# Neighbourhood attention on halves of the grid, with its values regrouped by transfers; a weight unit split in halves in the second mixer

## The reference

```python
s = einsum('brjqhd,brjuvhd->brjhquv', qg, k_win) * scale + bias
s = where(col_ok, s, -inf)      # 16 columns around the query's own
p = softmax(s over all kept keys)
o = einsum('brjhquv,brjuvhd->brjqhd', p, v_win)
```

## Time and profile before

| | before |
|---|---|
| median of 3 runs (lowest to highest) | 1637.62 us (1637.54 to 1637.75) |
| profiled execution, its own time | 1637.62 us |
| its span, first to last instruction | 1635.8 us |
| TensorE busy | 1625.7 us |
| VectorE, ScalarE, GpSimd busy | 937.8, 793.2, 149.5 us |
| mean granted TensorE clock | 0.999 |

### The profile page before, as it was taken

How to read it: one execution, slowest core, us unless ns; L and a number is a source line. 1 busy time by engine, 2 the same in 40 slices (tenths; PEclk the granted TensorE clock), 3 DMA queues, 4 the chain that set the end, 5 groups by cost and what they waited for, 6 DMA issues and landing times.

```text
span 1635.8 us, 20418 instructions
## 1 busy us (share of the span) xinstructions
PE 1625.7 (99%) x7642; PEld 1346.8 (82%) x7642; DVE 937.8 (57%) x900; ACT 793.2 (48%) x927; POOL 149.5 (9%) x197
## 2 busy tenths in 40 slices
PE   9999999999999999999999999999999999999998
PEld 7888888888888888888888888888888888888887
DVE  6454655675544645465566554477654457774455
ACT  6443455544444534445464443466544446554444
POOL 1001211011000000121101010031100002210000
PEclk9999999999999999999999999999999999999999
DMA  8777554447565667755444666561666564366562
GB/s 282 253 213 222 196 180 143 162 158 226 182 199 174 194 223 209 221 205 180 136 162 160 200 223 199 191 195 68 206 202 199 177 217 159 100 201 196 173 205 90
DMA packets 210099, 305.99 MB, mean 187 GB/s; under 512 B 11044, under 2 KB 153784, under 8 KB 210040
## 3 DMA queue, kind: packets, MB, share of 16 engines
q1 hardware_dynamic: 208616, 302.82, 56.7%
q0 software_dynamic: 1120, 1.86, 0.5%
q10 hardware_dynamic: 304, 0.50, 0.1%
HBM read 304.07 MB, written 2.88 MB: 188 GB/s over the span
## 4 chain that ended last, share of the span: by engine, by line
PE 96%; DVE 1%; POOL 1%; ACT 1%; SPq 0%; DMA 0%; issue 0%; POOLq 0%; ACTq 0%; DVEq 0%
PE pg L1860 20%; PE pg L1862 20%; PE pg L1861 20%; PE acc L1860 9%; PE acc L1862 9%; PE acc L1861 9%; PE pg L1979 2%; PE pg L1873 1%; PE acc L2065 1%; PE acc L2084 1%; DMA raw<-in_ffn_w_in 0%; PE acc L2072 0%; POOL work L856 0%; PE acc L2262 0%; PE acc L2220 0%
## 5 line engine op out<-in xcount | busy, mean ns | idle before, releaser
L1288 DVE TENSOR_TENSOR wlo<-raw,whi 128x2048 fp32r<-128x2048 f32 (+1 forms) x269 | 616.9, 2294 | 477.8 <-ACT whi L887 477.7
L887 ACT ACTIVATE whi<-raw 128x2048 fp32r<-128x2048 f32 (+1 forms) x269 | 513.2, 1909 | 323.8 <-PE acc L1862 157.6
L1860 PE MATMUL pg<-whi,xTh 128*128 128x512 f32 (+1 forms) x1456 | 576.5, 396 | 1.5 <-DVE xTl L1752 1.1
L1862 PE MATMUL pg<-whi,xTl 128*128 128x512 f32 (+1 forms) x1456 | 566.5, 389 | 0.0
L1861 PE MATMUL pg<-wlo,xTh 128*128 128x512 f32 (+1 forms) x1456 | 565.9, 389 | 0.0
L1860 PEld LDWEIGHTS pg<-whi,xTh 128*128 128x128 f32 x1456 | 273.7, 188 | 59.6 <-issue 1.7
L1862 PEld LDWEIGHTS pg<-whi,xTl 128*128 128x128 f32 x1456 | 273.4, 188 | 56.4
L1861 PEld LDWEIGHTS pg<-wlo,xTh 128*128 128x128 f32 x1456 | 273.8, 188 | 55.1 <-issue 1.4
L1860 PE MATMUL acc<-whi,bTh 128*128 128x512 f32 (+1 forms) x572 | 228.6, 400 | 0.0
L1862 PE MATMUL acc<-whi,bTl 128*128 128x512 f32 (+1 forms) x572 | 222.9, 390 | 0.0
L1861 PE MATMUL acc<-wlo,bTh 128*128 128x512 f32 (+1 forms) x572 | 221.8, 388 | 0.0
(11 more groups left out here) (238 smaller groups left out, 1074.6 us busy)
## 6 DMA issues: line engine op xcount, KB each, us to landing
raw<-in_ffn_w_in SPq DMA_DIRECT2D x172, 512.0 KB, 4.8
raw<-in_ffn_w_out SPq DMA_DIRECT2D x88, 512.0 KB, 4.3
raw<-in_w_gate_up SPq DMA_DIRECT2D x88, 512.0 KB, 4.6
raw<-in_mix_w_in SPq DMA_DIRECT2D x64, 512.0 KB, 4.4
raw<-in_w_down SPq DMA_DIRECT2D x44, 512.0 KB, 4.1
raw<-in_w_in SPq DMA_DIRECT2D x24, 512.0 KB, 4.6
raw<-in_mix_w_o SPq DMA_DIRECT2D x16, 512.0 KB, 4.4
raw<-in_w_o SPq DMA_DIRECT2D x16, 512.0 KB, 4.5
```

The source lines that it names most:

```text
L887: act_e.activation(whi[:, slot, 0:cols], raw[:, slot, 0:cols], ACT.Copy).then_inc(s.w_hi_ready, 1)
L1288: v.tensor_tensor(wlo[:, slot, 0:cols], raw[:, slot, 0:cols], f32(whi[:, slot, 0:cols]), ALU.subtract)\
L1860: pe.matmul(dst, xh, wh, start=first and i == 0, stop=False)
L1862: mm = pe.matmul(dst, xl, wh, start=False, stop=last and i == len(pairs) - 1)
```

## The change

In the first block's mixer a token tile of the attention is no longer 128 tokens in order (two grid rows), but one half of the grid: 4 rows by 32 columns. Such a half sees 4 x 40 keys instead of 256.

- `scores` has 2 x 4 x 40 = 320 columns (read from `kD` in pieces of 40), bias, maximum and exponentials too. The q copies write the halves' order; the mask and the bias transfers follow it (eight transfers per layer where there were four).
- The values are regrouped by transfers on SP's queue: `halve_values(t)` copies the 128 own keys of a half to `v_half` (4 transfers) and the 32 keys beyond it, for both heads of a pair on a block diagonal, to `v_edge` (8 transfers), which GpSimd zeroes first. SP issues the first after unit 11's load, the second after unit 13's and after the first `attend`.
- `scale(i-1)` on VectorE, between `refills(i+8)` and `add_gate_bias`, multiplies the probabilities by the inverse sums and sorts them in own keys (256 columns for the pair) and beyond (64). `probs_T` then waits for that and has three transposes. ScalarE copies the result in two pieces.
- `attend` has the values stationary and the turned probabilities moving: two products (128 keys, 64 channels, 128 queries) and one (64 rows for both heads' edges, 128 channels). The output comes out turned, so `normalise`, `attention_T` and `o_nat` go. ScalarE's and VectorE's `attended(t)` make `oTh` and `oTl`: t = 0 at the head of step 6, t = 1 after the loop.

In the second mixer the last addition of the convolution's second tile moves from GpSimd to VectorE, ahead of the split of unit 11. Unit 13 is split in two halves, ScalarE's both ahead of three of the group squares, VectorE's ahead of `scale_pair(1, .)` and between the two `pair_lo(1, .)`. The first half takes the place of count 12, and TensorE waits for the second half only in the middle of the first half block.

```diff
@@ SP, mixer_a
+                def halve_values(t):
+                    first, edge = t * HALF_W, (HALF_W, HALF_W - BEYOND)[t]
+                    for row in range(GRID_H):
+                        at, src = row % 2 * GRID_W, v_nat[:, row // 2, :]
+                        sp.dma_start(v_half[row * HALF_W:(row + 1) * HALF_W, t, :], src[at + first:at + first + HALF_W, :])\
+                            .then_inc(s.v_half_landed, 16)
+                    for row in range(GRID_H):
+                        at, src = row % 2 * GRID_W + edge, v_nat[:, row // 2, :]
+                        for e in range(2):
+                            to = e * EDGE + row * BEYOND
+                            dst = v_edge[to:to + BEYOND, t, :].rearrange("p (k e n) -> p e k n", k=4, e=2)[:, e]
+                            sp.dma_start(dst, src[at:at + BEYOND, :].rearrange("p (k e n) -> p e k n", k=4, e=2)[:, e])\
+                                .then_inc(s.v_half_landed, 16)
...
+                    if b == 5:
+                        sp.wait_ge(s.v_sb, 2 * l + 2)
+                        sp.wait_ge(s.qkT_tr, 4 * l + 4)
+                        sp.wait_ge(s.kd_zeroed, l + 1)
+                        halve_values(0)
+                    if b == 6:
+                        sp.wait_ge(s.na_o_done, 8 * l + 1)
+                        halve_values(1)
@@ VectorE, mixer_a
+                def scale(i):
+                    t, hp = i // 4, i % 4
+                    v.wait_ge(s.na_exp, 8 * l + i + 1)
+                    pair = na_inv[:, t, 2 * hp:2 * hp + 2]
+                    v.reciprocal(pair, na_sum[:, t, 2 * hp:2 * hp + 2]).then_inc(s.na_rinv, 1)
+                    v.wait_ge(s.na_rinv, 8 * l + i + 1)
+                    if i >= 1:
+                        v.wait_ge(s.naPT_done, 8 * l + i)
+                    p4 = probs[:, i % 2, :].rearrange("p (e r c) -> p e r c", e=2, r=GRID_H)
+                    own, beyond = ((0, HALF_W), (BEYOND, 0))[t]
+                    factors = pair.unsqueeze(2).unsqueeze(3)
+                    v.tensor_tensor(scaled[:, 0:T].rearrange("p (e r c) -> p e r c", e=2, r=GRID_H), p4[:, :, :, own:own + HALF_W],
+                                    factors.to_broadcast([P, 2, GRID_H, HALF_W]), ALU.mult)
+                    v.tensor_tensor(scaled[:, T:].rearrange("p (e r c) -> p e r c", e=2, r=GRID_H), p4[:, :, :, beyond:beyond + BEYOND],
+                                    factors.to_broadcast([P, 2, GRID_H, BEYOND]), ALU.mult).then_inc(s.na_scaled, 1)
...
                     if i == 6:
-                        normalise(0)
+                        attended(0)
                     if i < 9:
                         refills(i + 8)
+                    if 1 <= i <= 8:
+                        scale(i - 1)
@@ TensorE, mixer_a
-                    pe.matmul(acc[0][:, :], qT[:, hp, tok(t)], kD[:, hp, :, :], start=True, stop=True).then_inc(s.na_scores, 1)
+                    pe.matmul(acc[0][:, 0:2 * GRID_H * SEEN], qT[:, hp, tok(t)], seen(kD[:, hp, :, :], t), start=True, stop=True)\
+                        .then_inc(s.na_scores, 1)
 
                 def probs_T(i):
-                    pe.wait_ge(s.na_exp, 8 * l + i + 1)
+                    pe.wait_ge(s.na_scaled, 8 * l + i + 1)
                     for e in range(2):
-                        for kt in range(TT):
-                            at = e * T + kt * P
-                            tr = pe.transpose(acc[2][:, at:at + P], probs[:, i % 2, at:at + P], ident[:, :])
-                    tr.then_inc(s.naPT_done, 1)
+                        pe.transpose(acc[2][:, tok(e)], scaled[:, tok(e)], ident[:, :])
+                    pe.transpose(acc[2][0:2 * EDGE, T:T + P], scaled[:, T:T + 2 * EDGE], ident[:, :]).then_inc(s.naPT_done, 1)
...
-                            mm = pe.matmul(acc[3][:, h * NA_D:(h + 1) * NA_D], probsT[:, i % 2, at:at + P],
-                                           v_nat[:, kt, h * NA_D:(h + 1) * NA_D], start=kt == 0, stop=kt == 1)
-                    mm.then_inc(s.na_o_done, 1)
+                        pe.matmul(acc[3][e * NA_D:(e + 1) * NA_D, tok(hp)], v_half[:, t, h * NA_D:(h + 1) * NA_D],
+                                  probsT[:, i % 2, tok(e)], start=True, stop=False)
+                    pe.matmul(acc[3][:, tok(hp)], v_edge[:, t, tok(hp)], probsT[0:2 * EDGE, i % 2, T:T + P], start=False, stop=True)\
+                        .then_inc(s.na_o_done, 1)
@@ VectorE, mixer_b
+                v.wait_ge(s.conv_taps, 6 * l + 6)
+                v.tensor_tensor(convT[:, :, tok(1)], convT[:, :, tok(1)], taps[0], ALU.add).then_inc(s.conv_T, 1)
                 refills(11)
                 mla_out(1)
                 conv_out(1)
+                half_unit(13, 0)
                 scale_pair(1, 0)
                 scale_pair(1, 1)
-                skip(12)
-                refills(13)
                 pair_lo(1, 0)
+                half_unit(13, 1)
                 pair_lo(1, 1)
```

More of the change, by code:

```diff
@@ L101, in first_constants @@
     out[:, CA_DFT_C:CA_MASK] = np.concatenate([np.concatenate([even, odd]), np.concatenate([odd, even])], 1)
[L102 to L105, removed]
+    for half in range(TT):
+        col = half * HALF_W + np.arange(P) % HALF_W
+        start = np.clip(col - NA_COLS // 2, 0, GRID_W - NA_COLS)[:, None]
+        key = FIRST_SEEN[half] + np.arange(SEEN)[None, :]
+        at = CA_MASK + half * SEEN
+        out[:, at:at + SEEN] = np.where((key >= start) & (key < start + NA_COLS), 0.0, MASKED)
     return out
@@ L392, in build @@
         q_nat, k_nat = area(4096, TT, BANK), area(5120, TT, BANK)
-        o_nat = q_nat
+        v_half = area(4096, TT, BANK)
+        v_edge = work[0:2 * EDGE, 9216:9216 + TT * BANK].rearrange("p (t n) -> p t n", t=TT)
         v_nat, uf = area(6144, TT, BANK), area(7168, TT, BANK)
@@ L618, in attention_bias @@
                     sp.wait_ge(s.rpb_spread, LOADED * NA_DR * (l + 1))
[L619 to L623, removed]
+                    column = DEPTH * NA_H * NA_DR * GRID_W
+                    for row in (2 * r, 2 * r + 1):
+                        src = bass.AP(tensor=spread.tensor,
+                                      offset=t * HALF_W * column + l * (NA_H * NA_DR * GRID_W) + (GRID_H - 1 - row) * GRID_W,
+                                      ap=[[column, HALF_W], [NA_DR * GRID_W, NA_H], [1, T]])
+                        sp.dma_start(bias[HALF_W * row:HALF_W * (row + 1), t, :, :], src).then_inc(s.bias_landed, 16)
                 ffn("ffn1_w_in", "ffn1_w_out", l, r1,
@@ L1072, in mixer_a @@
                     sigmoid(3, t)
+                attended(1)
                 refills(17, 18, 19)
-                for t in range(TT):
-                    act_e.wait_ge(s.oT_tr, 2 * l + t + 1)
-                    copy(oTh[:, :, tok(t)], acc[2 * t][:, :].rearrange("p (c n) -> p c n", c=4), s.oT_hi)
                 refills(20, 21)
@@ L1464, in mixer_a @@
                 refills(3, 4, 5, 6)
-                def heads_T(n, dst, t, bank):
-                    v.wait_ge(s.qkT_tr, 4 * l + n + 1)
-                    v.tensor_copy(dst[:, :, tok(t)], bank[:, :].rearrange("p (c n) -> p c n", c=4)).then_inc(s.qkT_sb, 1)
                 for t in range(TT):
-                    heads_T(t, qT, t, acc[t])
+                    v.wait_ge(s.qkT_tr, 4 * l + t + 1)
+                    rows = acc[t][:, :].rearrange("p (k r h c) -> p h k r c", k=4, h=TT, c=HALF_W)
+                    for half in range(TT):
+                        at = half * P + t * 2 * HALF_W
+                        last = v.tensor_copy(qT[:, :, at:at + 2 * HALF_W].rearrange("p k (r c) -> p k r c", c=HALF_W), rows[:, half])
+                    last.then_inc(s.qkT_sb, 1)
                 v.wait_ge(s.kd_zeroed, l + 1)
@@ L1880, in split_ready, with half_block @@
                 pe.wait_ge(s.w_lo_ready, unit(slot, rnd) + 4)
-            def half_block(t, half, slot, rnd, n, bank, amid=None, first=0):
+            def half_block(t, half, slot, rnd, n, bank, amid=None, first=0, ready=None):
                 if t == 0:
-                    split_ready(slot, rnd)
+                    split_ready(*(ready or (slot, rnd)))
                 for k0 in range(0, 4, 2):
@@ L2382, in project @@
                         pe.wait_ge(s.xT_lo_ready, 4 * (o + 1) + 2 * k + t + 1)
-                    mm = half_block(t, 1 - k, u % SLOTS, rnd + u // SLOTS, BANK, out_b[n][t], amid, first=1)
+                    ready = None
+                    if u == 13 and t == 0:
+                        ready = (u - 1) % SLOTS, rnd + (u - 1) // SLOTS
+                        amid = lambda: split_ready(u % SLOTS, rnd + u // SLOTS)
+                    mm = half_block(t, 1 - k, u % SLOTS, rnd + u // SLOTS, BANK, out_b[n][t], amid, first=1, ready=ready)
                     if t == 1:
```

101 lines of the change are left out of this document (61 added, 40 removed).

## The result

The changed kernel takes 1647.22 us, median of 6 runs (1645.68 to 1649.14), beside 1637.58 us for the kernel before, 6 runs (1637.33 to 1637.97): a ratio of 1.0062, 95% interval 1.0051 to 1.0072. It is slower by 0.6%, above the forecast of 1638.5 and above the range of 1633.5 to 1644.

What follows compares the result with a forecast made beforehand. TensorE's instruction stream was taken to bound the kernel: 11.7 us of its work go and 14.5 us of waits come (+2.8), the second mixer gains 1.9, so 1637.6 + 2.8 - 1.9 = 1638.5 us, range 1633.5 to 1644.

Steps and rivals of the forecast that it cites:

- even steps: Even steps of the attention loop: TensorE waits 1.8 us per layer in all, added up from several small gaps.
- steps 3, 5 and 7: Odd steps of the attention loop: TensorE waits 1.2 us in each for the scaling queued behind VectorE's split.
- The price of the first scaling, 0.76 us: VectorE's scaling of the probabilities: reciprocal 0.20, 128x256 multiplication 0.34 to the next start, 128x64 one 0.21.
- First turn ... 244.76: Start of a layer's first probability transposes in the attention loop: 244.76 us, 1.21 later than before.
- Rival (3): Attention loop: scaling costs 1.1 instead of 0.76, or as much is lost in semaphores, every turn; 1642.9 us, chance 0.15.
- 6 x 0.108 = 0.65: Attend on TensorE: three products of 128 columns, six instructions at 0.108 us each, against 0.84 before.
- now three in 0.33: Transposes of probabilities on TensorE: three in 0.33 us per unit, where four took 0.44.
- 8.17 + x: Turn-to-turn time from even to odd step, before 7.62 + x: +0.55 us each; x is Fourier work after the turn.
- the second mixer's gain: Second mixer: moving the convolution addition and halving unit 13 gain 0.95 us per layer, 1.9 us in all.
- rival 4: Value regrouping on SyncE's queue lands late: at 1.5 us per transfer, 6 us late per layer, 1650.5 us; chance 0.06.
- Rival (1): Attention loop: scaling is ready before TensorE comes, so only the removed work counts; 1624 us, chance 0.05.
- removed work: TensorE work saved by scores, transposes, attend and dropped output turns: 5.84 us per layer, 11.7 for both.

Runs made afterwards that it cites:

- scale_first: The changed kernel with VectorE scaling unit i-1 ahead of the split of unit i+8 in every step; 1628.33 us, ratio 0.9943.
- pool_late: The changed kernel with GpSimd's Fourier additions held back until the layer's first scaling is done; 1640.36 us, ratio 1.0016.
- experiment 2: `pool_late` plus an unused VectorE maximum over 1792 bias columns ahead of each layer's first scaling; 1646.91 us. One more low-clock stretch was estimated at 1.6 us.
- wide_own_t1: `scale_first` with edge product and third transpose zero-padded to 128 rows, and own-key products to 128 columns in units 4 to 7; 1625.47 us, ratio 0.9925.

## Why the prediction was wrong

The mechanism was right: the scaling behind the split makes TensorE wait, the even steps too, and the gain in work is eaten. `scale_first` shows it with no wait and 18.9 us less. The waits are 14.5 us as forecast, but by chance: per layer 3.68 at the first turn where 1.85 was forecast, 0.96 in steps 3, 5 and 7 where 1.2 was, and 0.69 in even steps where 1.8 was (TensorE came later there, by the third term below). Three terms were wrong:

- **The price of the first scaling, 0.76 us.** "First turn ... 244.76" took the scaling from VectorE rows that stand alone. In step 1 GpSimd's Fourier additions run at that moment, and the two instructions take 2.5 us to the end. The first turn is 1.85 late per layer: 3.7 us. Rival (3) had a scaling of 1.1 in every turn as its case; it was dearer than that, but in one turn per layer. `pool_late` removes this and its consequence. The trace of before had the sign: in step 1 GpSimd's first addition of 512 columns began while VectorE's split ran and took 1.91, the next one 1.29, and in the earlier trace rows the 2.67 us of GpSimd's last addition, of 256 columns, stand beside a split too, where the one before it took 0.73.

```profile
243.50 1.91 POOL L755 TENSOR_TENSOR work<-work 128x512 f32<-128x512 f32 x1 [14.25 <-ACT work L1003]
...
245.48 1.29 POOL L757 TENSOR_TENSOR work<-work 128x512 f32<-128x512 f32 x1
...
1142.73 0.73 POOL L854 TENSOR_TENSOR work<-work 128x256 f32<-128x256 f32 x1
```

- **TensorE's clock after the wait**, which the sum put at nothing without a reason. 8.93 - 7.34 = 1.6 us in layer 0 of the profiled execution, and by the estimate of experiment 2 once more in the median one.
- **"6 x 0.108 = 0.65" and "now three in 0.33".** Attend takes 0.79. The turn takes 0.48 where TensorE doesn't wait, and 0.55 after a wait (0.44 for two, 0.11 for the third). These 0.36 show in full where TensorE sets the pace or the loop ends: the step from 1 to 2 is 7.34 in layer 1 (forecast 6.99), and from the last turn to the loop's end 313.84 - 306.59 = 7.25 (before 7.20, forecast 0.30 less). The steps from even to odd, where the turn alone counts, are 0.08, 0.14 and 0.10 above 8.17 + x. With the small differences of the other steps this is about 0.96 per layer, 1.9 us.

1638.5 + 3.7 + 1.6 + 1.9 = 1645.7, and the profiled execution took 1645.68. With the third term alone it is 1640.4, and `pool_late` took 1640.36. With a second low stretch it is 1647.3, beside the median of 1647.22.

The other steps held: the intervals from odd to even steps (3 to 4: 8.71, forecast 8.72; 5 to 6: 8.10 and 8.15; 7 to 8: 7.62 and 7.63), scores 0.54, the second mixer's gain, no wait of attend for the regrouping (rival 4), none for the copy after the loop. Rival (1) is right in its condition and wrong in its time: with no wait 1628.3 was reached, not 1624, since 0.14 in attend and 0.15 in the turn in 16 units are 4.6 us of "removed work" that was never removed. Of the two bounds given for attend, 0.43 and 0.87, the value lay near the upper one.

## What to carry to other kernels

A new instruction in a chain between engines goes ahead of the long work in its own queue that nobody waits for as soon: here the order of two calls was worth 18.9 us, between 0.6% slower and 0.6% faster than before. Price it in the company that it will have, by the timeline of the same stretch: GpSimd beside a VectorE instruction with two SBUF operands was worth 1.85 us at one place, and the lower clock behind that wait 1.6 more where it came. For small products count the changes of shape and not only the columns; padding with zeros to one shape was cheaper here, and the best kernel of these, `wide_own_t1`, is 0.75% faster than the kernel before.

## What the runs showed of the hardware that was not expected

- A VectorE multiplication of 64 columns took 0.22 us alone and 1.28 beside a GpSimd addition; one of 256 columns 0.42 and 1.29. GpSimd's addition of 512 columns took 1.29 alone and 1.87 beside VectorE's split.
- After waits of 3.7 us TensorE's granted clock was at 0.50 for about 3 us in three of four places, with about 1.6 us lost each; after waits of 1.7 us in neither of two.
- In a unit, going from the scores to products of 128 x 64 of stationary, from those to the edge product and, behind a 64 x 128 one, on to the transposes costs 0.14 to 0.20 us each time (0.25, 0.31 and 0.26 in the chain of waits for the first instruction behind the change, where 0.11 is the rule). A transpose with 64 columns of stationary costs none (0.11). The four passes of 64 columns gained 0.2 by lying side by side.
